# Moving the SBUF addresses of a TensorE-bound kernel: one place within 256 bytes for all moving tiles, another for all gate and up weights

## The reference

```
def _swiglu(h, w_gate, w_up, w_down):
    return (jax.nn.silu(h @ w_gate) * (h @ w_up)) @ w_down
...
x = x + 0.5 * _swiglu(_rmsnorm(x, g[0]), ffn_w_gate[layer, 0], ffn_w_up[layer, 0], ffn_w_down[layer, 0])
h = _rmsnorm(x, g[1])
...
x = x + mix.astype(x.dtype)
x = x + 0.5 * _swiglu(_rmsnorm(x, g[2]), ffn_w_gate[layer, 1], ffn_w_up[layer, 1], ffn_w_down[layer, 1])
```

## Time and profile before

| | |
|---|---|
| median of 3 runs | 2413.05 us (2412.19 to 2413.34) |
| the profiled execution | 2413.27 us |
| its span, first to last instruction | 2411.5 us |
| mean granted TensorE clock | 0.996 |
| TensorE busy | 2339.2 us, 97% |
| VectorE, ScalarE, GpSimd busy | 1738.6, 1144.1, 880.0 us |

### The profile page before, as it was taken

One profiled execution on the slowest core, in us unless ns is written; L12 is line 12 of the kernel. 1 busy time (PEld: TensorE's weight loads), 2 busy tenths in 40 slices (PEclk: granted clock), 3 DMA queues, 4 the chain that ended last, 5 costly groups with the idle time before them and its releaser, 6 DMA issues.

```text
span 2411.5 us, 42260 instructions
## 1 busy us (share of the span) xinstructions
PE 2339.2 (97%) x16963; PEld 1986.4 (82%) x16963; DVE 1738.6 (72%) x2296; ACT 1144.1 (47%) x1758; POOL 880.0 (36%) x533
## 2 busy tenths in 40 slices
PE   8999989999999999988999999999999999999999
PEld 6667768789899777876898998998987557898997
DVE  7999986496486489765874867856856776883871
ACT  5533353465364346244662654643644344662552
POOL 3799944322313456422114133132134212114123
PEclk9999999999999999999999999999999999999999
DMA  5222214233343432002334343342333221233333
GB/s 151 79 79 79 75 57 127 74 88 100 104 115 90 111 90 74 27 3 58 111 95 118 106 114 89 88 131 77 114 88 100 52 58 53 81 101 107 106 89 96
DMA packets 420791, 214.48 MB, mean 89 GB/s; under 512 B 17317, under 2 KB 419035, under 8 KB 420603
## 3 DMA queue, kind: packets, MB, share of 16 engines
q1 hardware_dynamic: 416523, 209.05, 30.6%
q10 hardware_dynamic: 4080, 2.83, 0.5%
HBM read 209.22 MB, written 2.10 MB: 88 GB/s over the span
## 4 chain that ended last, share of the span: by engine, by line
PE 73%; DVE 17%; issue 3%; ACT 3%; POOL 3%; DMA 0%; ACTq 0%; DVEq 0%; POOLq 0%
PE bank L995 10%; PE bank L1000 10%; PE bank L1003 10%; PE bank L344 9%; PE bank L341 9%; PE bank L337 9%; DVE bank L1690 4%; PE bank L1863 2%; PE bank L1860 2%; PE bank L1856 2%; DVE gu_w_lo L592 1%; POOL w_lo L319 1%; PE bank L3400 1%; PE bank L2748 1%; DVE hL L368 1%
## 5 line engine op out<-in xcount | busy, mean ns | idle before, releaser
L319 POOL TENSOR_TENSOR w_lo<-w_raw,w_hi 128x1024 fp32r<-128x1024 f32 (+5 forms) x276 | 532.9, 1932 | 613.1 <-ACT w_hi L311 611.3
L311 ACT ACTIVATE w_hi<-w_raw 128x1024 fp32r<-128x1024 f32 (+5 forms) x276 | 237.6, 861 | 623.2 <-PE bank L344 468.7
L592 DVE TENSOR_TENSOR gu_w_lo<-gu_w,gu_w_hi 128x1024 fp32r<-128x1024 f32 (+1 forms) x256 | 364.9, 1428 | 90.6 <-ACT gu_w_hi L583 90.0
L664 POOL TENSOR_TENSOR ffn_aL<-tmp,ffn_aH 128x512 fp32r<-128x512 f32 x88 | 134.5, 1529 | 725.7 <-ACT ffn_aH L708 725.7
L583 ACT ACTIVATE gu_w_hi<-gu_w 128x1024 fp32r<-128x1024 f32 (+1 forms) x256 | 302.9, 1185 | 3.1 <-DVE gu_w L566 3.1
L995 PE MATMUL bank<-hH,gu_w_hi 128*128 128x256 f32 x1280 | 203.7, 281 | 5.0 <-ACT tmp L700 5.0
L1000 PE MATMUL bank<-hL,gu_w_hi 128*128 128x256 f32 x1280 | 200.7, 279 | 0.0
L1003 PE MATMUL bank<-hH,gu_w_lo 128*128 128x256 f32 x1280 | 200.3, 278 | 0.0
L700 ACT ACTIVATE tmp<-bank 128x256 f32<-128x256 f32 x320 | 120.8, 378 | 165.7 <-PE bank L1003 165.7
L968 DVE TENSOR_TENSOR bank<-bank,R 128x512 f32<-128x512 f32 x64 | 44.8, 699 | 204.1 <-PE bank L344 203.6
L337 PE MATMUL bank<-ffn_aH,w_hi 128*128 128x512 f32 x704 | 181.1, 390 | 0.0
(11 more groups left out here) (553 smaller groups left out, 4684.6 us busy)
## 6 DMA issues: line engine op xcount, KB each, us to landing
gu_w<-in_ffn_w_gate SPq DMA_DIRECT2D x88, 512.0 KB, 3.7
gu_w<-in_ffn_w_up SPq DMA_DIRECT2D x88, 512.0 KB, 4.8
w_raw<-in_w_in SPq DMA_DIRECT2D x48, 512.0 KB, 3.8
w_raw<-in_ffn_w_down SPq DMA_DIRECT2D x64, 384.0 KB, 3.4
w_raw<-in_ffn_w_down SPq DMA_DIRECT2D x64, 320.0 KB, 3.2
w_raw<-in_even_w_in SPq DMA_DIRECT2D x26, 512.0 KB, 3.9
w_raw<-in_w_conv_out SPq DMA_DIRECT2D x8, 512.0 KB, 3.9
w_raw<-in_w_out SPq DMA_DIRECT2D x8, 512.0 KB, 3.9
```

The lines of the kernel that those rows point to most:

```text
L311: nc.scalar.activation(w_hi[u % 2][:, 0:K, :], w_raw[u % 4][:, 0:K, :], ACT.Identity).then_inc(w_hi_ready, 1)
L319: nc.gpsimd.tensor_tensor(w_lo[u % 2][:, 0:K, :], w_raw[u % 4][:, 0:K, :], w_hi[u % 2][:, 0:K, :].bitcast(F32), ALU.subtract).then_inc(w_l ...
L592: nc.vector.tensor_tensor(gu_wl[v % 3][:, b0:b1, :, :], gu_w[v % 3][:, b0:b1, :, :], gu_wh[v % 2][:, b0:b1, :, :].bitcast(F32), ALU.subtra ...
L664: nc.gpsimd.tensor_tensor(aL[:, in_half(n), :], up_t[:, :], aH[:, in_half(n), :].bitcast(F32), ALU.subtract).then_inc(a_lo, 1)
```

## The change

No instruction is added, removed or moved: on each of the five engines the rows of the two programs, waits included, are the same but for line numbers and the numbers of buffers, so no piece of the order is shown. What changes is where tiles lie. `par` (parameter columns, 408 of 416 used) goes to the front and `small` into its unused rest. That makes `xT`, and with it the ring, start at place 192, and lets `hH` follow the `tmp` tiles without a gap. The step of 128 in `place` is gone.

```diff
-            def place(self, r, step=256):
+            def place(self, r):
 
-                self.at += (r - self.at) % step
+                self.at += (r - self.at) % 256
                 return self.at
...
         m = Map(base0)
-        small = m.put("small", [P, 8])
-        m.place(64)
+        par = Map(m.at).put("par", [P, 408])
+        small = Map(m.at + 4 * 408).put("small", [P, 8])
+        m.at += 4 * 416
+        m.place(192)
         xT = m.put("xT", [P, DT, T])
...
-        par = m.put("par", [P, 416])
...
-        hH_at = m.place(ring_at)
+        hH_at = m.at
         GU_PLACE = hH_at - 64
...
-        u_at[1] = f_map.place(GU_PLACE, 128)
+        u_at[1] = f_map.place(GU_PLACE)
...
-        f_hi_at = f_map.place(hH_at, 128)
+        f_hi_at = f_map.place(hH_at)
```

## The result

The changed kernel takes 2421.61 us (median of 7 runs, 2419.56 to 2422.97) where the kernel before, on the same chip, takes 2413.05 (7 runs, 2410.74 to 2413.34): ratio 1.0035, 95% interval 1.0026 to 1.0044. It is slower, by 8.6 us. The forecast was 2401. The span of its profiled execution is 2421.1 us, against 2411.5 before, at about the same granted clock (0.995).

What follows compares the result with a forecast made beforehand. TensorE, busy 97%, was taken as the bound. Four second halves at -3.0 us each, all else 0, took 2413.3 to 2401.3, less 0.2 to the median: 2401 us, 8-in-10 range 2391 to 2421.

Steps and rivals of the forecast that it cites:

- item 2: Gate and up units: second halves enter short and stay so, 4 x -3.0 = -12 us; first halves left at 0.
- the ring's short pitch: Ring matmuls at 227 to 228 ns, read as twice the short 113.3 ns of gate and up matmuls.
- The sign of the step: Entry from ring to second half: weights 64 bytes above the moving tile before, 64 below after; no size of its own.
- P5 of unit v = 0: A product in a second half's first unit, moving 192 and weights 128, read as keeping the short pitch: 1.36 us.
- The throws from short to long: Gate and up units: jumps of the moving tile's place by 128 turn matmuls from 113.3 to 117.7 ns.
- Locked long: Rival: all gate and up units start long and nothing turns them back, +8 us, 2421 us; chance 0.30.
- No visible change: Rival: the mixture of short and long stays near today's, or places do not act, 2413 us within 5; chance 0.18.
- Item 1: Gate and up products, 80 units: 9.52 us each if short, 9.89 if long; all short -22 us, all long +8.
- Item 3: Ring units: moving and weights both go from 64 to 192, distance stays 0, so 0 us; +25 if 192 is bad.
- Item 4: Plain units: some 380 matmuls at 232 ns change by at most 5 ns, -2 to +1 us, taken as 0.
- Item 6: Weight loads: landing 4.8 us after issue, needed 9.5 us or more later, so cost 0 even if half as long again.
- Item 5: VectorE, ScalarE, GpSimd: operands move but the halves leave room; half a microsecond of possible added waits included in the range.

Runs made afterwards that it cites:

- w0: Changed kernel with all gate and up weights at place 0, moving tiles still at 192: 2418.77 us, ratio 1.0024 to the kernel before.
- all64: Changed kernel with every tile 128 bytes lower, moving tiles and ring at 64, gate and up weights at 0: 2420.26 us, ratio 1.0024 to before.
- w192: Changed kernel with all gate and up weights at place 192, the place of the moving tiles: 2436.61 us, ratio 1.0089 to the kernel before.
- hi128_low0_early: hi128_low0 with ScalarE's split of the gate and up weights issued earlier in a unit: 2400.67 us, ratio 0.9942 to the kernel before.
- hi128_low0: Changed kernel with low parts of the gate and up weights at place 0, high parts still at 128: 2415.4 us, ratio 1.0007 to the kernel before.
- one_low0: Changed kernel with only the weight buffer `gu_w1`, used every third unit, at place 0: 2415.1 us, ratio 1.0005 to the kernel before.
- early split: ScalarE's weight split issued ahead of the high part and later PSUM copies; ratios to before: 0.9987 on the kernel before, 1.0025 on the changed one.
- w64: Changed kernel with all gate and up weights at place 64, moving tiles still at 192: 2432.89 us, ratio 1.0079 to the kernel before.
- moving_jumps: Changed kernel with ring, `hH` and `hL` at 64, `st_hi` and `st_lo` at 192, all gate and up weights at 128: 2419.27 us, ratio 1.0022 to before.

## Why the prediction was wrong

The step that failed is item 2, "I take the second for the second halves": that behind the ring, with weights 64 bytes below the moving tile, the units would keep the ring's short pitch. All four second halves entered long instead, at 117.8 ns from the first group. Two readings under it failed with it.

- The sign of the step. I had set 64 above against 64 below. `w0` and `all64` show no difference between them in the second halves: both enter long. Nor did P5 of unit v = 0 keep anything at these places: it follows a long P6, and its own weights go from 128 (`gu_w_hi0`) to 0 (`gu_w0`). It was turned short at a jump of the weights, and such jumps are what the change removes.
- The ring's "short" pitch. Its 227 ns was read as twice the short one, hence a state to be kept. `w192` shows that the ring's distance of 0 gives 256 columns neither 113.3 nor 117.8 but 120.0. With the prediction's 106.7 ns for 256 columns that is 13 ns on top, and 227 ns is, as an estimate, 14 ns on top of twice 106.7: much the same for each matmul, not for each column. The ring is at another distance with levels of its own, and I take it that it had no short pitch to hand on. That the ring is what makes the halves enter long was not tried by itself.

The rest of item 2 held, and made the sign: "The throws from short to long are the moving tile's jumps, and they are removed; so are the throws back." The throws back were what before lived on. The rival "Locked long", held at 0.30, is what came: +8 us and 2421 us forecast for it, +8.6 and 2421.61 measured, halves of 108.8 us forecast, 108.8 to 108.9 measured. Its condition, fewer than 27% of the units short, was met: nearly none is. That is no luck: its shares, +4.4 us in the second halves and +3.6 in the first, came out as 4.5 and 4.1. "No visible change" is out, since the ratio's interval starts at 1.0026.

Item 1's prices (9.52 and 9.89 us a unit, 104.7 and 108.8 us a half) held: the changed kernel has the long one, hi128_low0_early the short one. Item 3 held in its sum: 227 ns at places 192 and 192, no bad place (`all64`). But `yH`, at 233 ns in all kernels, is no long state of the ring's distance: `yH` lies 64 below its weights. Item 4 held: the plain units went from 232 to 229 ns, about -1 us in its -2 to +1. Item 6 held: the halves show no wait for a load, though the loads land later than before:

```profile
gu_w<-in_ffn_w_up SPq DMA_DIRECT2D x88, 512.0 KB, 5.3
```

It was 4.8 us. In the kernels that have two or all of `gu_w0`, `gu_w1` and `gu_w2` at place 0 it is 4.8 or 4.9, in the others (64, 128 or 192) 5.2 or 5.3, so the place does cost the transfer up to half a microsecond.

Item 5 ("they have the room stated above") was right for this result, but wrong for the one I forecast. I read room from busy time, VectorE 87.8 of 107.7 us. The room ends with a loop of two engines at 9.77 us a unit, 0.12 us inside a long unit and 0.25 us outside a short one. Had the second halves entered short, they would by this have stumbled out of it within a few units, as hi128_low0 did: I do not think that the forecast of 2401 could have come true with ScalarE's order as it was. And the first halves, which I left at 0, went long too, for about half of the loss (4.1 of 8.6 us).

That the pitch is held is shown (one_low0, units at 113.3 ns with one place throughout). That ScalarE's order is what ends it in the second halves is shown by the pairs with and without the early split; that it does so through P4's late copy is read from the timelines, where the stumble at P4 is gone and the short pitch goes on. The order moves other work too, and no run delays that copy alone. Why a weights' jump turns the pitch in some stretches and not in others (part 1's first half), why one stumble turns it and another does not, and what physically holds it, stays open. Whether a jump of the weights the other way alone would do the same was not tried.

## What to carry to other kernels

- A tile's address can set the pitch of fp32r matmuls, and the pitch may depend on what ran before, not on the places alone. A change that takes away what throws it one way also takes away what throws it back: ask in which state it will be left, and count the entry and each wait as events.
- Before forecasting that one engine gets faster, work out the period of the loops that the others run with it, from the distance between two equal instructions; their busy share does not show it. Here 9.77 us stood behind 82% busy.
- Try a gain and the bound behind it together: the layout without the new order, and the new order without the layout, were each worth 0.1% or nothing, together 0.6%.

## What the runs showed of the hardware

- 256-column fp32r matmuls, each with its own weight load, at full clock: 113.3 or 117.8 ns at a distance of 64 between moving and weights, held for units on end; 120.0, or in some halves of `w64` 118.7, at a distance of 0 or 128.
- 512-column ones have other levels, and there the sign counts. Moving minus weights modulo 256, with the mean from start to start in the plain units: 0, 227 ns (w192); 64, 229 to 230 (changed kernel, all64); 128, 232 to 233 (w64); 192, 233 (w0, moving_jumps). The ring (0) has 227 and `yH` (192) 233 in all kernels. The kernel before, with both 64 and 192, has 232.
- The Trainium skill, "TensorE: Matmul & The Clock Gate", Part 2, has the weight load take nothing from the running matmul's reads. By that it should not matter how the two operands lie to each other; in these runs nothing but addresses differs between 117.8 and 120.0 ns, so the traces do not bear it out for these matmuls. Whether it is the weight load that takes something no run shows.
- VectorE's split of 1536 elements takes 1.76 us alone and 2.59 us in the early order, where GpSimd's subtraction (1.30 us) starts 0.33 us ahead of it. From one unit to the next VectorE then needs 9.56 to 9.57 us, with no idle time listed:

```profile
2264.89 1.30 POOL L667 TENSOR_TENSOR ffn_aL<-tmp,ffn_aH 128x512 fp32r<-128x512 f32 x1 [8.27 <-ACT ffn_aH L711]
2265.22 2.59 DVE L595 TENSOR_TENSOR gu_w_lo<-gu_w,gu_w_hi 128x1536 fp32r<-128x1536 f32 x1
...
2274.78 2.60 DVE L595 TENSOR_TENSOR gu_w_lo<-gu_w,gu_w_hi 128x1536 fp32r<-128x1536 f32 x1
```

  It is 0.04 to 0.05 us over a short unit. Over some units that adds up to the stumble at P3 of v = 8, where the copy that P3 waits for stands behind ScalarE's split; this is worked out from the two periods, and no run takes work off VectorE to try it. By it VectorE is the next bound. The page "SBUF — State Buffer" of the Trainium skill, section "Who interferes with whom", has a VectorE operation with two SBUF inputs contend with GpSimd's reads. This agrees: the 0.83 us more are nearly the 0.97 us that GpSimd's operation still had to run. Earlier in the same half, where VectorE's split starts first (2245.54, 1.74 us), it is GpSimd's operation that takes longer (2245.70, 2.73 us).
